# Two subtractions of every GLA level: on GpSimd instead of VectorE

## What is computed

```python
def gla_chunked(q, k, v, g, s0):        # q, k, g: (B, H, T, DK); v: (B, H, T, DV)
    def step(state, inp):
        qc, kc, vc, gc = inp
        b = jnp.cumsum(gc, axis=2)
        o_inter = jnp.einsum('bhid,bhde->bhie', qc * jnp.exp(b), state)
        diff = jnp.where(mask, b[:, :, :, None, :] - b[:, :, None, :, :], -jnp.inf)
        a = jnp.einsum('bhid,bhjd,bhijd->bhij', qc, kc, jnp.exp(diff))
        o = o_inter + jnp.einsum('bhij,bhje->bhie', a, vc)
        b_last = b[:, :, -1:, :]
        state = jnp.exp(b_last[:, :, 0, :])[..., None] * state + jnp.einsum('bhjd,bhje->bhde', kc * jnp.exp(b_last - b), vc)
        return state, o
```

## Time and profile before

| what | us |
|---|---|
| median of 3 runs | 2768.29 (2768.27 to 2769.61) |
| the profiled execution's own time | 2767.13 |
| its span in the profile | 2765.1 |
| TensorE busy in the span | 2713.4 (98%) |
| VectorE busy | 1576.5 (57%) |
| ScalarE busy | 853.5 (31%) |
| GpSimd busy | 75.3 (3%) |

### The profile page before, as it was taken

One profiled execution on the slowest core, in us unless ns is written; L12 is line 12 of the kernel. 1 busy time (PEld: TensorE's weight loads), 2 busy tenths in 40 slices (PEclk: granted clock), 3 DMA queues, 4 the chain that ended last, 5 costly groups with the idle time before them and its releaser, 6 DMA issues.

```text
span 2765.1 us, 33201 instructions
## 1 busy us (share of the span) xinstructions
PE 2713.4 (98%) x12906; PEld 2278.4 (82%) x12906; DVE 1576.5 (57%) x2135; ACT 853.5 (31%) x957; POOL 75.3 (3%) x150
## 2 busy tenths in 40 slices
PE   6999999999999999999999999999999999999999
PEld 5888878888888888888888887888899888888887
DVE  5735648735566458564763445677687632564433
ACT  3212225222242122321421324345555522332221
POOL 0000000000000000000000000000000000000000
PEclk9999999999999999999999999999999999999999
DMA  7644632635526446323273332212112333232232
GB/s 285 232 135 158 213 98 84 233 118 180 191 94 239 132 152 229 98 93 105 90 247 116 125 118 83 92 44 67 62 44 66 129 145 106 77 107 92 91 106 76
DMA packets 94662, 356.14 MB, mean 129 GB/s; under 512 B 10976, under 2 KB 12000, under 8 KB 85728
## 3 DMA queue, kind: packets, MB, share of 16 engines
q1 hardware_dynamic: 74848, 252.74, 27.4%
q0 software_dynamic: 19280, 101.23, 10.0%
q10 hardware_dynamic: 432, 0.75, 0.1%
HBM read 344.19 MB, written 8.39 MB: 128 GB/s over the span
## 4 chain that ended last, share of the span: by engine, by line
PE 89%; DVE 5%; ACT 2%; DMA 1%; issue 1%; SPq 1%; DVEq 0%; ACTq 0%
PE ps L1901 24%; PE ps L1902 24%; PE ps L1903 24%; PE ps L2086 3%; PE ps L2088 3%; PE ps L2087 3%; PE ps L2333 2%; DMA w_raw<-in_units 1%; PE ps L2278 1%; PE ps L2327 1%; SPq L508 1%; ACT w_hi L600 0%; PE ps L1921 0%; PE ps L1922 0%; PE ps L1923 0%
## 5 line engine op out<-in xcount | busy, mean ns | idle before, releaser
L1901 PE MATMUL ps<-h_hi,w_hi 128*128 128x512 f32 x1936 | 756.2, 391 | 5.1 <-DVE h_lo L1218 3.8
L1903 PE MATMUL ps<-h_hi,w_lo 128*128 128x512 f32 x1936 | 754.8, 390 | 0.0
L1902 PE MATMUL ps<-h_lo,w_hi 128*128 128x512 f32 x1936 | 754.8, 390 | 0.0
L600 ACT CAST w_hi<-w_raw 128x2048 fp32r<-128x2048 f32 (+1 forms) x240 | 422.6, 1761 | 610.5 <-PE ps L1903 518.1
L1082 DVE TENSOR_TENSOR w_lo<-w_raw,w_hi 128x2048 fp32r<-128x2048 f32 (+1 forms) x219 | 458.4, 2093 | 123.9 <-ACT w_hi L600 123.6
L1901 PEld LDWEIGHTS ps<-h_hi,w_hi 128*128 128x128 f32 x1936 | 364.2, 188 | 83.4 <-issue 6.9
L1903 PEld LDWEIGHTS ps<-h_hi,w_lo 128*128 128x128 f32 x1936 | 364.2, 188 | 75.7
L1902 PEld LDWEIGHTS ps<-h_lo,w_hi 128*128 128x128 f32 x1936 | 364.3, 188 | 75.1
L1901 PE MATMUL ps<-g_hi,w_hi 128*128 128x512 f32 x960 | 373.8, 389 | 0.0
L1903 PE MATMUL ps<-g_hi,w_lo 128*128 128x512 f32 x960 | 373.8, 389 | 0.0
L1902 PE MATMUL ps<-g_lo,w_hi 128*128 128x512 f32 x960 | 373.7, 389 | 0.0
(11 more groups left out here) (332 smaller groups left out, 2912.5 us busy)
## 6 DMA issues: line engine op xcount, KB each, us to landing
w_raw<-in_units SPq DMA_DIRECT2D x350, 512.0 KB, 4.5
ada<-in_ada_t POOLq DMA_DIRECT2D x56, 1024.0 KB, 6.5
w_raw<-in_units SPq DMA_DIRECT2D x128, 352.0 KB, 3.7
ada<-in_ada_t POOLq DMA_DIRECT2D x64, 512.0 KB, 5.0
ada_first<-in_ada_t SPq DMA_DIRECT2D x8, 1024.0 KB, 17.7
x_res<-in_x SPq DMA_DIRECT2D x4, 512.0 KB, 7.8
x_home<-x_res POOLq DMA_DIRECT2D x1, 2048.0 KB, 6.6
attn_tq<-attn_qx SPq DMA_DIRECT2D x32, 64.0 KB, 2.0
```

The lines of the kernel that those rows point to most:

```text
L600: nc.scalar.copy(W_HI[u.slot][:, 0:n], W_RAW[u.slot][:, 0:n]).then_inc(hi_done, 1)
L1901: pe.matmul(dst, hi[:, k, c], rhs_hi(k), start=(k == 0), stop=False)
L1902: pe.matmul(dst, hi[:, k, c], rhs_lo(k), start=False, stop=False)
L1903: last = pe.matmul(dst, lo[:, k, c], rhs_hi(k), start=False, stop=(k == kt - 1))
```

## The change

`level_d` moves from VectorE's list to GpSimd's, with the same two subtractions, tiles and semaphore `lv_d`. Its calls are gone from `rounds` on VectorE. On GpSimd they stand ahead of the waits for `at_made`: levels 0 to 4 ahead of the first store of a head, 5 and 6 ahead of the second. Two waits are added that VectorE's order gave before: level 0 waits for `b_made` (the cumulative sums), and levels 0 and 1 of a later head also wait for `o_ms`.

```diff
--- before.py
+++ after.py
@@ -581,8 +581,30 @@
 
             pool.wait_ge(x_made, KD)
             pool.dma_start(X_HOME, X[:]).then_inc(x_stored, 16)
+            def level_d(i, n):
+                sz = LEVELS[n]
+                nb = T // (2 * sz)
+
+                mid = BB[:, 0:2 * TA + 2].rearrange("p (d x) -> p d x", d=2)[:, :, 0:T] \
+                    .rearrange("p d (n r) -> p d n r", r=2 * sz)[:, :, :, sz - 1:sz].broadcast_to([P, 2, nb, sz])
+                b = BB[:, 0:2 * TA].rearrange("p (d x) -> p d x", d=2)[:, :, 0:T].rearrange("p d (n r) -> p d n r", r=2 * sz)
+                e = EL[n % 2]
+                e_kq = e[:].rearrange("p d (n r) -> p d n r", r=2 * sz)
+                e_qk = e[:, ::-1, :].rearrange("p d (n r) -> p d n r", r=2 * sz)
+                if n == 0:
+                    pool.wait_ge(b_made, 2 * i + 2)
+                if n >= 2:
+                    pool.wait_ge(lv_mm, len(LEVELS) * i + n - 1)
+                elif i > 0:
+                    pool.wait_ge(o_ms, i)
+                    pool.wait_ge(o_stored, 16 * 2 * i)
+                nc.gpsimd.tensor_tensor(e_kq[:, :, :, 0:sz], b[:, :, :, 0:sz], mid, ALU.subtract)
+                nc.gpsimd.tensor_tensor(e_qk[:, :, :, sz:2 * sz], b[:, :, :, sz:2 * sz], mid, ALU.subtract).then_inc(lv_d, 1)
+
             for i in range(GH_):
                 for m in range(2):
+                    for n in ((0, 1, 2, 3, 4), (5, 6))[m]:
+                        level_d(i, n)
                     pool.wait_ge(at_made, 4 * i + 2 * m + 2)
                     pool.dma_start(AT_HOME[:, 2 * i + m, :], AT_S[:]).then_inc(at_stored, 16)
                 for e in range(2):
@@ -1571,23 +1593,6 @@
                         nc.vector.scalar_tensor_tensor(ST[d][:, c, :], ST[d][:, before, :], T1[d][:, col:col + 1],
                                                        PS[:, (n - 1) * DV:n * DV], ALU.mult, ALU.add).then_inc(st_made, 1)
 
-            def level_d(i, n):
-                sz = LEVELS[n]
-                nb = T // (2 * sz)
-
-                mid = BB[:, 0:2 * TA + 2].rearrange("p (d x) -> p d x", d=2)[:, :, 0:T] \
-                    .rearrange("p d (n r) -> p d n r", r=2 * sz)[:, :, :, sz - 1:sz].broadcast_to([P, 2, nb, sz])
-                b = BB[:, 0:2 * TA].rearrange("p (d x) -> p d x", d=2)[:, :, 0:T].rearrange("p d (n r) -> p d n r", r=2 * sz)
-                e = EL[n % 2]
-                e_kq = e[:].rearrange("p d (n r) -> p d n r", r=2 * sz)
-                e_qk = e[:, ::-1, :].rearrange("p d (n r) -> p d n r", r=2 * sz)
-                if n >= 2:
-                    dve.wait_ge(lv_mm, len(LEVELS) * i + n - 1)
-                elif i > 0:
-                    dve.wait_ge(o_stored, 16 * 2 * i)
-                nc.vector.tensor_tensor(e_kq[:, :, :, 0:sz], b[:, :, :, 0:sz], mid, ALU.subtract)
-                nc.vector.tensor_tensor(e_qk[:, :, :, sz:2 * sz], b[:, :, :, sz:2 * sz], mid, ALU.subtract).then_inc(lv_d, 1)
-
             def level_k(i, n):
                 dve.wait_ge(lv_e, len(LEVELS) * i + n + 1)
                 nc.vector.tensor_tensor(EL[n % 2][:], KQ[:, :, 0:T], EL[n % 2][:], ALU.mult).then_inc(lv_k, 1)
@@ -1668,19 +1673,16 @@
 
             def rounds(i):
                 row_max(i, 0)
-                level_d(i, 0)
                 normalise(i, 0)
 
                 row_max(i, 1)
                 level_k(i, 0)
                 normalise(i, 1)
-                level_d(i, 1)
 
                 row_max(i, 2)
                 level_out(i, 0)
                 level_k(i, 1)
                 normalise(i, 2)
-                level_d(i, 2)
                 split_lo(at(U_G + 4 * i + 3))
                 attended(i, 0)
 
@@ -1688,27 +1690,23 @@
                 level_out(i, 1)
                 level_k(i, 2)
                 normalise(i, 3)
-                level_d(i, 3)
 
                 row_max(i, 4)
                 level_out(i, 2)
                 level_k(i, 3)
                 normalise(i, 4)
-                level_d(i, 4)
                 attended(i, 1)
 
                 row_max(i, 5)
                 level_out(i, 3)
                 level_k(i, 4)
                 normalise(i, 5)
-                level_d(i, 5)
                 states(i, 0)
 
                 row_max(i, 6)
                 level_out(i, 4)
                 level_k(i, 5)
                 normalise(i, 6)
-                level_d(i, 6)
                 split_lo(at(U_G + 4 * i + 4))
                 attended(i, 2)
 
```

## The result

| kernel | median us | runs |
|---|---|---|
| before | 2768.29 (2767.46 to 2769.61) | 9 |
| after | 2775.14 (2773.61 to 2779.59) | 9 |

The ratio is 1.0029, with a 95% interval of 1.0020 to 1.0038, which is 5.5 to 10.5 us; the two medians lie 6.85 us (0.25%) apart. The profiled execution of after took 2778.31 us with a span of 2776.3, one of the longest of its runs; that of before took 2767.13 with 2765.1.

What follows compares the result with a forecast made beforehand. TensorE was taken to bound the kernel, so the removal gains 0. Added waits of 3.8 (first head), 6.6 (later heads) and 0.4 (rounds) sum to 10.8 us, giving 2779 us, 0.4% slower; range 2767.5 to 2788.

Steps and rivals of the forecast that it cites:

- What bounds the kernel, and the worth of what was removed: GLA stage: TensorE bounds; taking 38.4 us of subtractions off VectorE gains 0, with 3.0 us the most possible.
- The end of the bounds at 0.95: One 512-column GpSimd subtraction takes 0.95 us if two inputs are fetched one after the other and writing is hidden.
- The mechanism: At the shared memory port, VectorE instructions stand still while GpSimd subtracts, priced at 1.15 us an instruction.
- First head, 3.8 us: GpSimd's four subtractions delay VectorE's twelve scalings of `DIAG_K`; TensorE loses 4.4 - 0.65 = 3.8 us.
- the last scaling ends 4.4 us late: First head: four subtractions, 4.6 us from 1783.2, fall on the twelve scalings and delay the last by 4.4 us.
- Later heads, 2.2 us each: Beginnings of heads two to four: VectorE delayed 4.25 us, less its 2.06 us query DMA wait; 6.6 us for three.
- So 4.25 push VectorE's list: Later heads: of GpSimd's 4.6 us, 0.35 lie ahead of `decay_arg` at 1905.36; the other 4.25 us delay VectorE.
- second rival: VectorE's row keeps the port, GpSimd enters only at pauses: about 1 us a later head, 2771.6 us; chance 0.15.
- Against it: at 1905.0 GpSimd would come first: Objection to the rival of VectorE keeping the port: at later heads GpSimd is ready at 1905.0, ahead of VectorE's 1905.36.
- The upper bound of 3.6 a head: Later heads, all four subtractions in one go: ScalarE's `decay_in` 4.2 us late, TensorE loses 3.6 a head, 10.8 for three.
- Rounds, 0.4 us: GpSimd's level 2 pair delays VectorE's small product by 0.3 us; about 0.1 us of TensorE wait in each of four heads.
- The clock: First head: a new wait of 3.8 us could bring a half-clock stretch, up to 3.4 us more on top.

Runs made afterwards that it cites:

- the rounds alone: Against after, levels 0 and 1 of each head are subtracted on VectorE again, levels 2 to 6 stay on GpSimd: 2767.71 us, ratio 1.0001 to before.
- the beginnings alone: Against before, only levels 0 and 1 of each head are subtracted on GpSimd, the others stay on VectorE: 2775.55 us, ratio 1.0028.
- the kernel without any GpSimd work: Before plus one unused maximum over 1024 columns on VectorE at the beginning of heads 2 to 4: 2770.84 us, ratio 1.0012.

## Why the prediction was right, and where its sizes were off

The forecast was 2779.0, the measured median is 2775.14: slower, inside the range, and less slow than forecast.

- **What bounds the kernel, and the worth of what was removed.** Right. The 38.4 us off VectorE were worth nothing: the kernel with the rounds alone has 40 of the 56 subtractions off VectorE's list and stands at 1.0001.
- **The duration on GpSimd.** 1.15 us was taken, 1.03 to 1.16 measured. The end of the bounds at 0.95, two inputs in a row and the writing hidden, was the nearer one for all levels but one. The page "GPSIMD Engine Reference" of the Trainium skill, section "Performance versus the Vector engine", led to an estimate of 1.12, which lies inside the measured durations.
- **The mechanism.** Right, and shown: exclusion, which costs TensorE at heads' beginnings, with GpSimd's reads, and for the scalings its writes as well.
- **First head, 3.8 us.** The mechanism was right, the size of "the last scaling ends 4.4 us late" was not: 2.93. The subtractions began behind `split_lo`, as forecast, but the four took 4.0 us instead of 4.6, and four of the twelve scalings (0.8 us of work) got in between them. With the clock as in before the wait is 2.2 us (2.15 with the beginnings alone) and not 3.8. That after shows 3.75 all the same is due to the half-clock stretch, which lies ahead of the wait in before and behind it in after, for a loss of 4.3. The agreement with the forecast is luck. Holding these subtractions back gained about 3.
- **Later heads, 2.2 us each.** This is the term that was mis-sized: 1.0 to 1.3 measured. The step that failed is "So 4.25 push VectorE's list". It would hold if GpSimd, once ready, held the port for four instructions or stopped VectorE for each of them in turn. In the second head VectorE's row kept GpSimd out for 3.8 us, and GpSimd did much of its work in the 2.06 us in which VectorE waits for the DMA: the second rival's mechanism, and its 1 us a head. That rival's own working doesn't give the figure, though: one or two instructions of 1.15 us less the wait of 2.06 are 0.2 at most. The 1.1 came out because GpSimd's last two subtractions lay behind the DMA wait. "Against it: at 1905.0 GpSimd would come first" was also too sure: it came 0.21 us behind. Where it did come first, in the fourth head, VectorE got in between its instructions and was 3.3 us late, 1.3 after the DMA wait. The upper bound of 3.6 a head, by way of ScalarE's `decay_in`, names the path by which that head lost its 1.3, but it left out the slack on it: 3.3 us of delay made a wait of 1.24.
- **Rounds, 0.4 us.** 0 in after, 0.6 in the trace of the kernel with the rounds alone: right in kind and in size. The small product was slowed there (0.68 us; 0.29 in after), as forecast. By the prediction's own rows there would have been no wait: 0.3 us on top of 1833.32 is 1833.62, still ahead of 1833.68. At half a microsecond the slack was used up.
- **The sum.** With the sizes measured it is 2.3 to 4.3, by the clock, and 3 x 1.15: 5.8 to 7.8, and 6.85 by the medians. It lies between the forecast's 10.8 and the second rival's 3.3: that rival was right for the later heads, the forecast for the first one.
- **The clock.** I priced a half-clock stretch as an addition in the first head alone, up to 3.4 us. There one was moved, none was added, and the one at 1807.70 was half as long in after. "Behind a stretch with little to do" also misreads what lay ahead of that one: TensorE was busy for all 10 us from 1790 and for 5.7 of the next 7, and the stretch began 0.7 us behind the end of a wait of 1.3 us. Those that were added came in the later heads, behind waits of 1.8 us, 1.6 us each and not in every execution: in the profiled one of after there are two, 3.1 us, and it lies 3.2 above its median. That it is these two that lift it above the median isn't shown, since the other executions have no profile.

## What to carry to other kernels

Before moving work to an engine that shares a way into memory, list what the other one does at the moment when the moved work becomes ready, not on average: here 56 moved instructions cost 7 us through the 16 that became ready where VectorE was the engine that TensorE waited for, and nothing that could be told through the other 40. "As soon as the buffer is free" is then the wrong time: in the first head, the same work held back to where VectorE has slack cost nothing that could be told. In the later heads it was left where it was, and an earlier place in VectorE's list for the instruction that TensorE waits for took the cost away. And work taken off an engine that isn't the bound gives at most the waits that end in it, which the table of waits states before anything is built.

## What the runs showed of the hardware that I had not expected

- **The exclusion isn't fair.** When VectorE was first, a row of its instructions without a pause kept GpSimd out for as long as it lasted: 3.8 us in the second head; in a round, too (the subtraction of level 3 behind `split_lo`):

```profile
1839.56 2.47 POOL L601 TENSOR_TENSOR gla_el<-gla_b 128x512 f32<-128x512 f32 x1 [3.20 <-PE ps L2276]
...
1838.79 2.28 DVE L1104 TENSOR_TENSOR w_raw_lo<-w_raw,w_hi 128x2048 fp32r<-128x2048 f32 x1
```

  When GpSimd was first, they took turns, instruction by instruction. In the six traces with all or the first subtractions on GpSimd there are 18 beginnings of later heads. In the four in which GpSimd came 0.10 to 0.40 us ahead of `decay_arg` the engines took turns; in the other 14 it came later, or ahead by 0.04 at most, and VectorE's row ran through. Both cost TensorE about the same here.
- **A profile's GpSimd duration holds the time that it stood still:** 4.85 us for an instruction that takes 1.03. The start of the next instruction behind it, less 1.03, tells about when it really ran.
- **A short wait can cost nearly twice its length.** Behind waits of TensorE of 1.7 to 1.8 us the granted clock fell to 0.50 for 3.4 us in 5 of 12 cases, 1.5 to 1.6 us each, in the kernel without any GpSimd work as well. What decides it in one execution and not in the next stays open, and so does why the stretch at 1780 is missing in some traces; no run here tells.
